# A Mamba-2 mixer's loop in another order, with the decay's exponent made by four Relu on the scalar engine

## The reference, cut to what matters

```
z, xbc, dt_raw = split(h @ w_in)                    # z: 16 blocks of 128 features
xs, B, C  = split(silu(causal_conv(xbc) + bias))    # 8 groups, 4 heads each, state 128
dt = softplus(dt_raw + dt_bias);  a = -exp(a_log)
cs   = cumsum(dt * a)                               # within a chunk of tokens
decay[l,s] = exp(cs[l] - cs[s])  for s <= l, else 0
y_diag = ((C B^T) * decay) @ (dt * xs)
states = B^T (exp(cs_end - cs) * dt * xs);  y_off = exp(cs) * C @ state_before
y = (y_diag + y_off + D * xs) * silu(z)
y = rms_normalize(y, per group) * norm_g;   out = y @ w_out
```

## Time and profile before

| | |
|---|---|
| time, median of 3 runs | 3390.54 us (3389.55 to 3393.44) |
| the profiled execution | 3387.45 us, of which the span of the trace is 3385.6 us |
| busy, share of the span | PE 87%, DVE 63%, PE's weight loads 61%, ACT 42%, POOL 19% |
| granted PE clock, mean | 0.955 |
| the mixer's loop and its end, 831 to 1081 us of the span | PE 213.2 of 250 us, DVE 183.8, ACT 163.6, POOL 35.3 |

### The profile page before, as it was taken

One profiled execution on the slowest core, in us unless ns is written; L12 is line 12 of the kernel. 1 busy time (PEld: TensorE's weight loads), 2 busy tenths in 40 slices (PEclk: granted clock), 3 DMA queues, 4 the chain that ended last, 5 costly groups with the idle time before them and its releaser, 6 DMA issues.

```text
span 3385.6 us, 34615 instructions
## 1 busy us (share of the span) xinstructions
PE 2949.5 (87%) x12002; PEld 2051.8 (61%) x12002; DVE 2123.0 (63%) x3960; ACT 1407.5 (42%) x2884; POOL 656.6 (19%) x572
## 2 busy tenths in 40 slices
PE   6989999899988899998988797978879777777777
PEld 5868888687766688887777653656547332223222
DVE  7654443587776444432552879879678888655555
ACT  3243222434666432223733367772443433333333
POOL 0000000000111000000000032334453444434442
PEclk8999999999999999999999898989989899999999
DMA  6544444243112344442202497898999899999997
GB/s 249 184 140 138 138 145 144 89 150 118 51 57 94 112 130 137 148 132 99 98 28 88 180 344 282 346 372 353 411 420 419 349 422 421 421 422 421 422 421 331
DMA packets 147548, 797.82 MB, mean 236 GB/s; under 512 B 16304, under 2 KB 18480, under 8 KB 81712
## 3 DMA queue, kind: packets, MB, share of 16 engines
q0 software_dynamic: 73728, 536.90, 39.0%
q1 hardware_dynamic: 69840, 251.69, 22.7%
q10 hardware_dynamic: 3808, 7.02, 0.6%
HBM read 793.46 MB, written 2.10 MB: 235 GB/s over the span
## 4 chain that ended last, share of the span: by engine, by line
PE 52%; DVE 19%; DMA 19%; ACT 6%; issue 4%; POOL 0%; DVEq 0%; SPq 0%; POOLq 0%; ACTq 0%
PE psum L153 52%; DMA tail<-in_experts,tail 18%; DVE tail L187 5%; DVE tail L170 2%; DVE tail L182 2%; ACT L164 2%; ACT arena L164 2%; DVE arena L182 1%; DVE region L170 1%; DVE tail L193 1%; ACT tail L164 1%; DVE tail L190 1%; DVE tail L205 1%; DVE tail L196 1%; DVE rounded L170 1%
## 5 line engine op out<-in xcount | busy, mean ns | idle before, releaser
L153 PE MATMUL psum<-tail,arena 128*128 128x256 f32 (+2 forms) x3580 | 1270.3, 504 | 264.7 <-ACT arena L164 235.1
L153 PE MATMUL psum<-rounded,rounded 128*128 128x512 f32 x5496 | 1278.9, 393 | 41.0 <-DVE rounded L182 22.6
L153 PEld LDWEIGHTS psum<-rounded,rounded 128*128 128x128 f32 x5496 | 1034.5, 189 | 262.3 <-issue 38.1
L153 PEld LDWEIGHTS psum<-tail,arena 128*128 128x128 f32 x3580 | 673.2, 198 | 815.6 <-issue 756.9
L216 POOL DMA_INDIRECT tail<-in_experts,tail x512 | 590.0, 1152 | 1225.0 <-PE psum L153 754.0
L187 DVE CUSTOM_DVE_ANT_0 tail<-tail 128x1024 f32<-128x1024 f32 x512 | 621.0, 1223 | 316.6 <-DMA tail<-in_experts,tail 315.5
L164 ACT ACTIVATE tail<-tail 128x1 f32<-128x1 f32 (+1 forms) x1056 | 266.3, 252 | 775.4 <-DVE tail L187 738.4
L170 DVE TENSOR_TENSOR rounded<-arena,rounded 128x1024 fp32r<-128x1024 f32 (+2 forms) x285 | 316.2, 1110 | 331.6 <-ACT rounded L164 331.4
L164 ACT ACTIVATE rounded<-arena 128x1024 fp32r<-128x1024 f32 (+2 forms) x317 | 292.0, 939 | 407.6 <-DVE arena L170 232.5
L164 ACT ACTIVATE arena<-psum 128x256 f32<-128x256 f32 (+2 forms) x210 | 97.3, 479 | 398.2 <-PE psum L153 397.5
L170 POOL TENSOR_TENSOR arena<-arena 128x512 f32<-128x512 f32 x32 | 46.9, 1464 | 1104.7 <-ACT arena L164 1104.7
(11 more groups left out here) (85 smaller groups left out, 1557.9 us busy)
## 6 DMA issues: line engine op xcount, KB each, us to landing
arena<-in_ada SPq DMA_DIRECT2D x136, 512.0 KB, 3.7
arena<-in_fin SPq DMA_DIRECT2D x88, 512.0 KB, 4.3
arena<-in_win SPq DMA_DIRECT2D x56, 512.0 KB, 3.3
arena<-in_fout SPq DMA_DIRECT2D x32, 512.0 KB, 3.8
arena<-in_mxbc SPq DMA_DIRECT2D x32, 512.0 KB, 4.2
arena<-in_pq SPq DMA_DIRECT2D x32, 512.0 KB, 7.8
arena<-in_ain SPq DMA_DIRECT2D x24, 512.0 KB, 5.0
arena<-in_mz SPq DMA_DIRECT2D x16, 512.0 KB, 3.8
```

Source lines behind the costliest of these rows:

```text
L153: return self.e.matmul(o, a, b, start=start, stop=stop, skip_group_check=skip)
```

## The change

The exponent min(cs[l] - cs[s], 0) was made by a subtraction and a minimum on DVE for all four heads at once. Now ACT makes max(cs[s] - cs[l], 0) with one Relu for each head (bias = a column of `cstok`, scale -1, read from the bank "sg"), and its Exp gets scale -1. On DVE two instructions of 128 x 512 leave each iteration, on ACT four of 128 x 128 come in.

The loop's order changes on each engine. The z halves run three iterations earlier (n = 0 to 31), and nothing of z is left behind the loop. The squares and their sum stay at n = 8, 12, ..., but the statistic moves to n + 1 and the root to n + 2. The two scalings of a pair go to n + 3 and n + 5, one in each. On ACT the squares move behind a(n). On DVE `dve_ssd_b(n - 2)` and with it its wait for PE moves behind a(n); weights(n - 1) stays first. On POOL a pair's sum moves behind the iteration's `xw`. One more weight piece is prepared inside the mixer (`made=1`), and one fewer behind it.

```diff
-            e.tt(quads(segb[p]), quads(ps[k2]), cstok[:, c, hs].unsqueeze(2).broadcast_to([128, 4, 128]),
-                 ALU.subtract).then_inc(*s_seg.tick(n))
             e.tt(cbm[p], ps[k1][:, 0:128], tri, ALU.mult)
-            e.wait_ge(*s_seg.at(n))
-            e.ts(segb[p], segb[p], 0.0, ALU.min).then_inc(*s_min.tick(n))
...
+            for r in range(4):
+                rs = slice(128 * r, 128 * r + 128)
+                h = 4 * g + r
+                ins = e.act(segb[p][:, rs], ps[k2][:, rs], ACT.Relu, bias=cstok[:, c, h:h + 1], scale=-1.0)
+            ins.then_inc(*s_fall.tick(n))
             e.act(ceb[p], ps[k2], ACT.Exp).then_inc(*ps.release(k2))
-            e.wait_ge(*s_min.at(n))
-            e.act(segb[p], segb[p], ACT.Exp).then_inc(*s_exp.tick(n))
+            e.wait_ge(*s_fall.at(n))
+            e.act(segb[p], segb[p], ACT.Exp, scale=-1.0).then_inc(*s_exp.tick(n))
...
-        second_of = lambda n: (n - 4) // 2 if n > 3 and n % 2 == 0 else None
-        gate_of = lambda n: (n - 5) // 2 if n > 4 and n % 2 else None
-        norm_of = lambda n: (n - 8) // 4 if n > 7 and n % 4 == 0 else None
-        apply_of = lambda n: norm_of(n - 1)
-        round_of = lambda n: range(4 * (n - 32), 4 * (n - 31)) if n >= 32 else ()
+        second_of = lambda n: (n - 1) // 2 if 0 < n < 32 and n % 2 else None
+        gate_of = lambda n: (n - 6) // 2 if n > 5 and n % 2 == 0 else None
+        squares_of = lambda n: (n - 8) // 4 if n > 7 and n % 4 == 0 else None
+        stat_of = lambda n: squares_of(n - 1)
+        root_of = lambda n: squares_of(n - 2)
+        apply_of = lambda n: (n - 11) // 2 if n > 10 and n % 2 else None
...
-                if n > 2:
-                    pe_z(e, (n - 3) // 2, FRONT if n % 2 else BACK)
+                    pe_z(e, n // 2, BACK if n % 2 else FRONT)
                 if n > 1:
                     pe_ssd_b(e, n - 2)
-                if norm_of(n) is not None:
-                    pe_norm_pair(e, norm_of(n), RG)
+                if stat_of(n) is not None:
+                    pe_norm_pair(e, stat_of(n), RG)
...
+            for n in range(32):
                 if n > 1:
                     act_ssd_b(e, n - 2)
                 if second_of(n) is not None:
                     act_z(e, second_of(n))
-                if n < 32:
-                    act_ssd_a(e, n)
...
+                act_ssd_a(e, n)
+                if squares_of(n) is not None:
+                    act_pair_squares(e, squares_of(n))
+                if root_of(n) is not None:
+                    act_pair_root(e, root_of(n))
                 if second_of(n) is not None:
                     act_ahead(e)
...
+            act_o(e, range(0, 4))
+            act_pair_squares(e, 6)
+            act_o(e, range(4, 8))
+            act_pair_squares(e, 7)
+            act_pair_root(e, 6)
             act_ahead(e)
...
+            act_o(e, range(8, 14))
+            act_pair_root(e, 7)
             act_o(e, range(14, 16))
...
+                if n < 32:
+                    dve_ssd_a(e, n)
+                if second_of(n - 1) is not None:
+                    dve_after(e, pc["z", second_of(n - 1)])
                 if n > 1:
                     dve_ssd_b(e, n - 2)
```

More of the change, by code:

```diff
@@ L612, in pe_out, with act_out @@
                 pe_stat(e, ("post", i, 7), stat, ones, False, True)
-        def act_out(e, i, groups):
+        def act_out(e, i, groups, made=0):
             for kk in range(8):
-                for k0, nk in groups:
+                for k0, nk in groups[0 if kk else made:]:
                     act_ahead(e)
@@ L630, in act_y, with dve_out @@
             e.act(yT[:, kk, :], ps["y", i, kk], ACT.Copy, scale=post(i, kk)).then_inc(*ps.release(("y", i, kk)))
-        def dve_out(e, i, groups):
+        def dve_out(e, i, groups, made=0):
             dve_derived_post(e, i)
@@ L635, in dve_out @@
                 for k0, nk in groups:
-                    dve_ahead(e)
+                    if kk or k0 >= 8 * made:
+                        dve_ahead(e)
                     dve_after(e, pc["out", i, kk, k0])
@@ L999, in pool_ssd @@
             for n in range(33):
-                if norm_of(n) is not None:
-                    pool_pair_sum(e, norm_of(n))
                 g, c = ITS[n] if n < 32 else (0, 3)
[L1003 to L1010, removed]
+                if c < 3:
+                    p = n % 3
+                    e.wait_ge(*s_xdt.at(n))
+                    if n >= 3 and ITS[n - 3][1] < 3:
+                        e.wait_ge(*s_st.at(n - 3))
+                    e.tt(quads(xw[p]), quads(xdt[p]), wtok[:, c, 4 * g:4 * g + 4].unsqueeze(2).broadcast_to([128, 4, 64]),
+                         ALU.mult).then_inc(*s_xw.tick(n))
+                if squares_of(n) is not None:
+                    pool_pair_sum(e, squares_of(n))
             pool_pair_sum(e, 7)
@@ L1080, in act_pair_squares, with dve_apply @@
                 act_square(e, ("zn", g, u), xs[:, 2 * g + u, :])
-        def dve_norm_pair(e, g):
+        def dve_apply(e, kk):
+            g = kk // 2
             e.wait_ge(*rs_ok.at(("zn", g)))
[L1084 to L1087, removed]
+            e.stt(xs[:, kk, :], xs[:, kk, :], cc("mng", kk), rst[g % 2], ALU.mult, ALU.mult).then_inc(*n_ok.tick(kk))
         def pe_z(e, kk, own):
@@ L1138, in act_ssd, with act_pair_root @@
                     act_z(e, second_of(n))
-                if n < 32:
-                    act_ssd_a(e, n)
-                if norm_of(n) is not None:
-                    act_rstd(e, ("zn", norm_of(n)), ("zn", norm_of(n), 1), 256, rst[norm_of(n) % 2])
+                act_ssd_a(e, n)
+                if squares_of(n) is not None:
+                    act_pair_squares(e, squares_of(n))
+                if root_of(n) is not None:
+                    act_pair_root(e, root_of(n))
                 if second_of(n) is not None:
                     act_ahead(e)
-                act_o(e, round_of(n))
-            act_z(e, 15)
+            act_o(e, range(0, 4))
[3 more added lines that the diff above has]
+            act_pair_root(e, 6)
             act_ahead(e)
[L1148 to L1151, removed]
+            act_o(e, range(8, 14))
+            act_pair_root(e, 7)
             act_o(e, range(14, 16))
+        def act_pair_root(e, g):
+            act_rstd(e, ("zn", g), ("zn", g, 1), 256, rst[g % 2])
         def dve_ssd(e):
-            for n in range(34):
-                if 0 < n < 33:
+            for n in range(33):
+                if n:
                     dve_ssd_weights(e, n - 1)
+                if n < 32:
+                    dve_ssd_a(e, n)
+                if second_of(n - 1) is not None:
+                    dve_after(e, pc["z", second_of(n - 1)])
                 if n > 1:
                     dve_ssd_b(e, n - 2)
-                if n < 32:
-                    dve_ssd_a(e, n)
                 if gate_of(n) is not None:
@@ L1164, in dve_ssd @@
                 if apply_of(n) is not None:
-                    dve_norm_pair(e, apply_of(n))
+                    dve_apply(e, apply_of(n))
                 if second_of(n - 1) is not None:
                     dve_ahead(e)
-                    dve_after(e, pc["z", second_of(n - 1)])
-                dve_o(e, round_of(n))
-            dve_z(e, 15)
+            dve_o(e, range(0, 4))
+            dve_ssd_b(e, 31)
+            for kk in (14, 15):
+                dve_z(e, kk)
+            dve_o(e, range(4, 8))
+            for kk in (11, 12, 13):
+                dve_apply(e, kk)
             dve_ahead(e)
-            dve_after(e, pc["z", 15])
             dve_o(e, range(8, 14))
-            dve_norm_pair(e, 7)
+            for kk in (14, 15):
+                dve_apply(e, kk)
             dve_o(e, range(14, 16))
@@ L2494, in act_program @@
             act_ssd(e)
-            act_out(e, 2, MGROUPS)
+            act_out(e, 2, MGROUPS, made=1)
             act_pre(e, 3)
@@ L2522, in dve_program @@
             dve_ssd(e)
-            dve_out(e, 2, MGROUPS)
+            dve_out(e, 2, MGROUPS, made=1)
             dve_derived(e, 3)
```

15 lines of the change are left out of this document (6 added, 9 removed).

## The result

The changed kernel took 3408.12 us (median of 4 runs, 3406.07 to 3410.62) against 3390.05 us for the kernel before on the same chip (4 runs, 3388.10 to 3393.44). The ratio is 1.0052, with a 95% interval of 1.0040 to 1.0064: slower, and the forecast was 3408.

A forecast was written before the change was run, and what follows sets the result against it. PE bounds the kernel, so the wait ending last on it counts. Bank waits, z-half waits, low clock and the uncovered end made the stage 19 us later; added to the 3390.54 median, slightly reduced: 3408 us, range 3399 to 3416 (0.65).

The forecast's parts named there:

- Part 1: Exponent: DVE loses 1.1 us an iteration, 35 in all; ACT gains four Relu, 1.04 us, ahead of both Exp.
- Part 2: Statistic's bank: PE can't start the next a until ACT's Ln has read the statistic; 5.0 us, six times.
- Part 3: Behind the z half: Silu's wait sits on the table load, delaying DVE's state; 0.8 us per group, plus early waits.
- the 3432 of the rival: Table switches at twice the row's length, each of three loads 1.3 us longer, 4 us a group: 3432; chance 0.02.
- Part 4: PE's clock falls to 1.2 GHz behind each 5.0 us wait; 2.0 us each time, ends 1.4 and 2.7.
- the sum: All stage terms added from a(0)'s start at 831.10: stage ends at 1100.2 instead of 1081.07, 19 us later.
- Part 5: Covered work: DVE's relief gains nothing, since ACT is last; POOL's sums and weight pieces are ready ahead of need.
- Part 6: Behind the loop no z work fills PE; a chain through DVE and ACT lasts 41.6 us from a(31)'s start.
- A: Rival, faster: Ln done before PE needs the bank, PE becomes the bound, groups of 24.6 us: 3370; chance 0.07.
- B: Rival, no change: bank wait with everything at its lower end, Relu 0.65, clock 1.4: 3394.5; chance 0.14.
- C: Rival, slower still: more waits or longer low clock, 1.5 us a group and 3 at the end: 3420; chance 0.12.

The follow-up runs named there:

- e4: e3 with `ceb` times C on DVE moved behind `dve_ssd_b`, so the state's addition and the modulation sum's release come ahead of it; 3363.01 us, ratio 0.9922.
- e3: The changed kernel with ACT's root at the head of its iteration, ahead of the state's copy that waits for PE; 3381.48 us, ratio 0.9979.
- e7: e4 with the exponent made on DVE by subtraction and minimum, as in the kernel before, not by Relu on ACT; 3358.64 us, ratio 0.9908.
- e2: The changed kernel's new order, with the exponent left on DVE as in the kernel before; 3391.73 us, ratio to the kernel before 1.0003.
- e1: The kernel before in its old order, with only the exponent changed to four Relu on ACT; 3390.67 us, ratio 1.0005.
- e5: The changed kernel with the Silu's two waits swapped, so the table load no longer waits for the z product; 3398.88 us, ratio 1.0027.

## Why the prediction was right, step by step

**Part 1, the exponent: right.** The groups of ACT's instructions between 829 and 1090 us (busy us, mean ns) have 377 ns for a Relu, where 0.36 us was forecast; the start of the next Exp is 1.00 us behind the first Relu, against 1.04.

```profile
L164 ACT ACTIVATE region<-psum,region 128x128 f32<-128x128 f32 x128 | 36.4, 377 | 0.0
L164 ACT ACT_TABLE_LOAD x47 | 60.3, 1283 | 34.0 <-PE psum L153 33.3
```

**Part 2, the bank: right where it stood, mis-sized in two groups.** Forecast: the Ln's end 10.4 us behind the start of the a before, PE's next start at 10.5, and of this a gap of 5.0. Measured: 10.2 (951.13 to 961.33), 10.25 (to 961.38), and a gap of 4.68. The timeline of PE over that iteration, ahead of the row at 961.38 (a, and b's last matmuls):

```profile
951.13 1.05 PE L153 MATMUL psum<-arena,region 128*128 128x128 f32 x8
...
955.42 1.29 PE L153 MATMUL psum<-region 128*64 128x128 f32 x10
```

In the two groups with a modulation sum the step failed in its place and came near in its size. It had the second half of one a waiting for 5.0 less 1.0. Measured were three waits: 1.40 for ACT, 2.79 for the modulation sum's own bank and 0.24 or 0.73 for the Ln. DVE releases that sum, and in the new order it stands behind `ceb` times C and so behind ACT; the prediction followed the ring of banks for the statistic only, and e4, which moves this release ahead, shows the wait gone. The sums are close by luck: 4.4 and 4.9 measured, 4.0 forecast.

**Part 3, behind the z half: right.** 0.69 measured in each group, 0.8 forecast. The four early waits were forecast as 0.6, 0.7, 1.6 and 0.7 and came as 0.59, 0.69 (855.59), 1.60 and 0.69 (880.67); the first and the third (timeline of PE, the changed kernel):

```profile
840.58 3.01 PE L153 MATMUL psum<-rounded,rounded 128*128 128x512 f32 x12 [0.59 <-ACT arena L164]
...
868.59 1.29 PE L153 MATMUL psum<-region 128*64 128x128 f32 x10 [1.60 <-DVE region L182]
```

From the load at 959.35 to the Ln at 960.64 are 1.29 us, from 970.46 to 971.75 again 1.29. The Trainium skill ("ScalarE: Activation LUTs", What ACT_TABLE_LOAD costs) has 2.66 us with a drain; by that figure, as an estimate, the chain of part 2 would have ended near 962.7, and the kernel near the 3432 of the rival. The measurement decides against it.

**Part 4, the clock: right in kind, a little high for most waits, too low in two places.** It fell behind each of the four waits of 4.68. At 961.38 a whole a took 2.79 us (to 964.17) in place of 1.36, and the z half behind it 3.19 in place of 2.93: 1.7 us, forecast 2.0, between the ends of 1.4 and 2.7. A group thus lasted 30.8 us and not 31.6: 0.3 less for the clock, 0.3 for the gap, 0.1 for the state's wait, and 0.1 less work than was read off. Behind the last of the four, at 1058.11, the z half took 4.24 us, and the clock cost 2.7. In the first group with a modulation sum it fell once, and in the second twice, from 1016 and from 1026 us on, and there it cost some 5 us where the sum had one term of 2.0; this group, from 1004.80 to 1039.96, lasted 35.2 us and not 31.4. One of its z halves (timeline of PE, the changed kernel):

```profile
1028.11 5.27 PE L153 MATMUL psum<-rounded,rounded 128*128 128x512 f32 x12
```

**Part 5, what is covered: right by the times.** The 32.5 us that DVE lost, forecast as 35, brought nothing. It waits for ACT instead: 108.2 us from 829 to 1085 us, where the same line of the kernel before has 12.3. Inside the loop PE has no wait for POOL or for a weight piece, as forecast (waits: sum, count, longest):

```profile
DVE region L170 <- ACT region L164: 108.2, 25, 9.2
```

**Part 6, the end: right in its sum, and partly by luck.** T, the start of a(31), was to be 1058.6 and is 1058.11. But a(0) began 1.14 us earlier than the sum has it; from there to T are 228.2 us, forecast 227.5. In these, three groups were 0.8 us short each and the second with a modulation sum 3.8 long, so that errors of part 4 cancelled. The chain behind it was to end at T + 41.6; DVE's weight piece, its last step, ends at 1100.18, T + 42.1 (timeline of DVE, the changed kernel). On PE the chain showed first as a wait of 4.88 us ahead of the last y's (1071.80), which the prediction had within DVE's 15.7 and didn't name.

```profile
1098.95 1.23 DVE L170 TENSOR_TENSOR rounded<-arena,rounded 128x1024 fp32r<-128x1024 f32 x1 [0.18 <-ACT rounded L164]
```

PE began its undisturbed run a piece earlier, at 1098.09, and not with that last piece. By the start of the 192 matmuls the stage lost 18.4 us, from its own start 19.5, where the sum had 19.1.

**The rivals.** A (PE the bound, 3370) did not come; its condition, a bank released before PE asks for it, is what e3 brings about, and e4 and e7 even end below its 3370. A still had 3.6 us of early waits and 0.8 in each of five groups, where e4 shows 0.58 early and none for the state inside the loop; that is 7 us. e4 also has two waits of 1.40 that A lacks, and a shorter wait ahead of the last y's (3.48 for 4.88); how the rest divides was not worked out. B (3394.5) needed all terms at their lower ends. Its term for the Relu was far off (1.00 measured, not 0.65), its clock was 0.3 too low for most waits and more for the others. C's further waits did not come; its longer low clock did, in one group and behind the last bank wait.

## What to carry to other kernels

Work moved to an idle engine costs what its place in a chain costs, not its time: the same four Relu an iteration cost 16 us where they stood in nearly every chain that PE waited for, some 4 us where PE still waited for such a chain in three places, and nothing measurable in the old order, where they took the place of a wait of ACT for DVE. When an order is changed, look on each engine for an instruction that waits for the bounding engine and stands ahead of the release of something that this engine needs; moving one call out from behind such a wait was worth 27 us here. And two parts that each measure as no change need not add up to none: both halves gave 1.000 here, and together 1.005.

## What the runs showed of the hardware that was not expected

The clock didn't follow the length of the wait alone. In the changed kernel it fell behind each wait of 4.68 us. In e2 it fell behind the waits of 3.65 us at 926.27, 956.47 and 1043.12, where eight matmuls took 2.08 us, but not at once behind the one at 985.32: there eight took 1.16, and the z half behind them 4.54 and not 3.0. In e1 it fell in the same way behind one wait of 2.14 us (968.82), and not behind the next (997.60). In e4 it had fallen behind a wait of only 1.40 (985.99, 2.08 us for eight), while the same wait at 888.31 left it full, 1.16. It can also fall before the wait ends: from 1057 to 1058 us in the changed kernel the granted clock was 0.50, and PE's next matmul began at 1058.11. What else decides can't be told from these runs, and no run tried it.

Which of two waits of an ACTIVATE sits on the table load ahead of it was decided by the order in which they were written, and the swap alone shortened the stage by 6.7 us (e5 against the changed kernel; 9.2 us between the medians).
